# First norm of a two-layer backbone kernel on Trainium2: sum of squares, reciprocal and two tile splits ahead of the last scale tiles, the K/V block queued ahead of the last two tiles

## What is computed

```python
def rmsnorm(x, g):
    xf = x.astype(jnp.float32)
    y = xf * lax.rsqrt(jnp.mean(xf * xf, axis=-1, keepdims=True) + EPS)
    return (y * g.astype(jnp.float32)).astype(x.dtype)

def modulation(cond, w_mod, b_mod):
    m = jax.nn.silu(cond) @ w_mod + b_mod
    return jnp.split(m, 6, axis=-1)
...
        sh1, sc1, g1, sh2, sc2, g2 = [m[:, None, :] for m in modulation(c, w_mod[layer], b_mod[layer])]
...
        h = rmsnorm(x, norm1_g[layer]) * (1 + sc1) + sh1
        proj = h @ w_in_l
```

## Time and profile before

| | |
|---|---|
| median of three runs | 2337.09 us |
| profiled execution, own time | 2338.05 us |
| its span (first to last instruction) | 2336.3 us |
| TensorE busy in the span | 2217.6 us, 95% |
| VectorE busy | 1727.9 us, 74% |
| ScalarE busy | 1132.2 us, 48% |
| mean granted TensorE clock | 0.977 |
| data moved by DMA | 513.89 MB, mean 220 GB/s |

### The profile page before, as it was taken

How to read it: one execution, slowest core, us unless ns; L and a number is a source line. 1 busy time by engine, 2 the same in 40 slices (tenths; PEclk the granted TensorE clock), 3 DMA queues, 4 the chain that set the end, 5 groups by cost and what they waited for, 6 DMA issues and landing times.

```text
span 2336.3 us, 33202 instructions
## 1 busy us (share of the span) xinstructions
PE 2217.6 (95%) x12554; PEld 1868.1 (80%) x12554; DVE 1727.9 (74%) x2384; ACT 1132.2 (48%) x1502; POOL 42.7 (2%) x84
## 2 busy tenths in 40 slices
PE   7989999997999999789997999999999999999998
PEld 6754776655777777657986999999999999999997
DVE  6776587646666766776736888888888888888886
ACT  3315221213333232434324766767676666767675
POOL 0000000000000000000000000000000000000000
PEclk9998999999999999889997999999999999999999
DMA  7500144343444443312535898989898998989895
GB/s 302 183 30 1 68 155 161 127 144 119 160 152 162 144 144 126 116 43 78 183 123 215 318 355 306 361 303 359 311 353 325 337 359 303 361 303 358 311 348 194
DMA packets 61296, 513.89 MB, mean 220 GB/s; under 512 B 6963, under 2 KB 8115, under 8 KB 21045
## 3 DMA queue, kind: packets, MB, share of 16 engines
q1 hardware_dynamic: 49716, 471.16, 54.0%
q0 software_dynamic: 11520, 41.95, 5.0%
HBM read 512.03 MB, written 1.05 MB: 220 GB/s over the span
## 4 chain that ended last, share of the span: by engine, by line
PE 87%; DVE 7%; ACT 2%; issue 2%; DMA 1%; SPq 0%; DVEq 0%; ACTq 0%
PE bank L752 9%; PE bank L754 9%; PE bank L753 9%; PE bank L505 5%; PE bank L506 5%; PE bank L507 5%; PE bank L617 5%; PE bank L768 4%; PE bank L769 4%; PE bank L770 4%; PE bank L627 4%; PE bank L461 2%; PE bank L673 2%; PE bank L659 2%; PE bank L649 2%
## 5 line engine op out<-in xcount | busy, mean ns | idle before, releaser
L1448 DVE TENSOR_TENSOR m_low<-W,m_high 128x2048 fp32r<-128x2048 f32 x225 | 515.7, 2292 | 126.1 <-ACT m_high L1000 126.1
L752 PE MATMUL bank<-m_high,gathered_high 128*128 128x256 f32 x1792 | 508.7, 284 | 13.8 <-DVE m_low L1448 12.4
L754 PE MATMUL bank<-m_low,gathered_high 128*128 128x256 f32 x1792 | 507.7, 283 | 0.0
L753 PE MATMUL bank<-m_high,gathered_low 128*128 128x256 f32 x1792 | 507.0, 283 | 0.0
L1000 ACT ACTIVATE m_high<-W 128x2048 fp32r<-128x2048 f32 x225 | 431.9, 1920 | 8.2 <-issue 7.9
L752 PEld LDWEIGHTS bank<-m_high,gathered_high 128*128 128x128 f32 x1792 | 342.7, 191 | 25.2 <-DVE m_low L1448 14.8
L753 PEld LDWEIGHTS bank<-m_high,gathered_low 128*128 128x128 f32 x1792 | 342.7, 191 | 8.0
L754 PEld LDWEIGHTS bank<-m_low,gathered_high 128*128 128x128 f32 x1792 | 342.7, 191 | 0.0
L1451 DVE TENSOR_TENSOR m_low<-W,m_high 128x1024 fp32r<-128x1024 f32 x225 | 274.4, 1219 | 0.0
L505 PE MATMUL bank<-h_high,tile_high 128*128 128x512 f32 (+1 forms) x704 | 259.1, 368 | 11.7 <-DVE tile_low L1178 11.7
L1002 ACT ACTIVATE m_high<-W 128x1024 fp32r<-128x1024 f32 x225 | 237.2, 1054 | 6.8 <-PE bank L770 6.8
(11 more groups left out here) (216 smaller groups left out, 3559.2 us busy)
## 6 DMA issues: line engine op xcount, KB each, us to landing
W<-in_moe SPq DMA_DIRECT2D x225, 1536.0 KB, 8.3
W<-in_w_mod_later POOLq DMA_DIRECT2D x80, 512.0 KB, 3.6
W<-in_ffn SPq DMA_DIRECT2D x33, 1024.0 KB, 4.8
W<-in_attn_blocks SPq DMA_DIRECT2D x24, 1280.0 KB, 5.8
W<-in_attn_blocks SPq DMA_DIRECT2D x22, 1024.0 KB, 5.1
W<-in_attn_blocks SPq DMA_DIRECT2D x8, 1536.0 KB, 6.9
shift_tiles<-in_w_mod_first SPq DMA_DIRECT2D x8, 512.0 KB, 14.0
scale_tiles<-in_w_mod_first SPq DMA_DIRECT2D x8, 512.0 KB, 14.8
```

The lines of the kernel that those rows point to most:

```text
L752: mm(b[:, 0:256], hgh[:, k, :], m13h[:, u % 2, k, :], start=k == 0, stop=False)
L753: mm(b[:, 0:256], hgl[:, k, :], m13h[:, u % 2, k, :], start=False, stop=False)
L754: last = mm(b[:, 0:256], hgh[:, k, :], m13l[:, u % 2, k, :], start=False, stop=k == KD - 1)
L1448: tt(m13l[:, u % 2], chunk[u][:, 0:2 * D].rearrange("p (k n) -> p k n", k=KD), m13h[:, u % 2].bitcast(F32), ALU.subtract).then_inc(S("moe_ ...
```

## The change

1. SyncE queues block 0 (K and V) ahead of shift tile 7 and scale tile 7; at its old place, after scale tile 7, nothing is issued for it.
2. TensorE does `sum_squares` of the first norm after scale tile 5 instead of after tile 6.
3. VectorE adds the squares two at a time ahead of shift tiles 3, 4 and 5, instead of 5, 6 and 7.
4. VectorE no longer waits for the scale after shift tile 7. It goes on to `attention_half`, takes the reciprocal, splits tiles 0 and 1, and only then waits for `mod_scale_full`, adds the bias and makes the gain (`first_scale`).
5. ScalarE takes the root first and then makes the high parts of tiles 0 and 1.
6. Tile 2 (q0) is split after the norm's units on both engines, and ahead of clearing `ypad`. This holds in layer 1 as well, where tiles 0 and 1 stay ahead of the norm.

```diff
@@ SyncE @@
             for j in range(KD):
+                if j == KD - 1:
+                    sp.dma_start(slots[0][:, 0:BLOCK_LEN[0]], attn_in[0, 0, :, 0:BLOCK_LEN[0]]).then_inc(S("block_in0"), 16)
                 sp.dma_start(shift0[:, j], first_in[j]).then_inc(S(f"shift_tile_in{j}"), 16)
...
-                    sp.dma_start(slots[s][:, 0:n], attn_in[layer, idx, :, 0:n]).then_inc(S(f"block_in{s}"), 16)
+                    if layer or idx:
+                        sp.dma_start(slots[s][:, 0:n], attn_in[layer, idx, :, 0:n]).then_inc(S(f"block_in{s}"), 16)
@@ TensorE, modulation @@
-                    if j == KD - 2:
+                    if j == 5:
                         pe.wait_ge(S("cs_row_ready"), 4)
                         sum_squares(0, "norm1", T)
@@ ScalarE, norm @@
                 fn(root[:, 0:n], b[:, 0:n], ACT.Sqrt, bias=C("eps"), scale=1.0 / D).then_inc(free(layer, name), 1)
+                if layer == 0 and name == "norm1":
+                    for t in range(2):
+                        split(layer, t)
@@ ScalarE and VectorE, attention_half @@
-                for n in range(TILE_RING):
-                    split(layer, n)
+                if layer:
+                    for n in range(2):
+                        split(layer, n)
                 norm(layer, "norm1", T)
+                split(layer, 2)
@@ VectorE, modulation @@
-                    if j >= 5:
-                        for k in range(1 + 2 * (j - 5), 3 + 2 * (j - 5)):
+                    if 3 <= j < 6:
+                        for k in range(2 * j - 5, 2 * j - 3):
                             add_square(0, "norm1", k, T)
...
+                dve.wait_ge(S("mod_shift_ready"), KD)
+
+            def first_scale():
+
                 bias = vec[:, 0, KD:2 * KD].unsqueeze(2).broadcast_to([P, KD, 2])
                 dve.wait_ge(S("mod_scale_full"), 1)
                 tt(modT[:, 0, KD:2 * KD, :], banks[4][:, 0:2 * KD].rearrange("p (q v) -> p q v", v=2), bias, ALU.add) \
                     .then_inc(S("mod_scale_read"), 1)
                 dve.wait_ge(S("mod_scale_read"), 1)
-                dve.wait_ge(S("mod_shift_ready"), KD)
+                gains(0, "norm1")
@@ VectorE, norm @@
                 step(dve.reciprocal(rstd[:, 0:n], root[:, 0:n]))
+                if layer == 0 and name == "norm1":
+                    for t in range(2):
+                        split(layer, t)
+                    first_scale()
@@ VectorE, main @@
             modulation()
-            gains(0, "norm1")
```

## The result

The changed kernel is faster, and by more than forecast. Its median over seven runs is 2324.68 us, against 2337.09 us over seven runs of the kernel before in the same rounds: ratio 0.9957, 95% interval 0.9946 to 0.9969. (The two medians alone would give 0.9947; the ratio lies nearer to that of the means, 2327.2 and 2336.8 us, because the median falls into the faster of two groups.) Forecast were 2330.6 us, with a range down to 2328.6 us. The seven runs are not spread evenly, though. Four lie at 2324.06, 2324.23, 2324.61 and 2324.68 us, three at 2330.61, 2330.7 and 2331.5 us. Two later runs gave 2330.72 and 2330.9 us. Of nine runs of the same kernel four are near 2324.4 us and five near 2330.8 us, and the forecast hits the second group. So there are two things to explain: the start, and the 6.3 us between the groups.

A forecast was written before the change was run, and what follows sets the result against it. The start was taken to be bound by order: VectorE stood still 5.56 us for the last scale matmul. 6.7 us gained there less 0.2 us in layer 1 gave 6.5 us, median 2330.6 us, range 2328.6 to 2333.8 us.

The forecast's parts named there:

- The scale's wait is an order, not work; the first unit moves from 49.99 to 43.29 us: End of the start: splits and reciprocal need no scale, so the norm's first unit comes 6.70 us earlier.
- Nothing below 43.19 us is possible here: Norm's first unit: the scale's end at 42.53 us plus 0.66 us for bias and gain caps the gain at 6.8 us.
- TensorE's matmuls cost nothing more or less, the squares come 3 us early, the high parts hide behind the reciprocal: Start: scale still ends at 42.51 us, squares at about 29.2 us, ScalarE's high parts at 38.7 us with 1.6 us to spare.
- The two transfers delayed cost nothing: Start: shift tile 7 and scale tile 7 land behind block 0 with 0.8 and 4 us to spare, so zero cost.
- Tile 2 behind the norm, layer 0: Layer 0's first norm: tile 2 is ready for TensorE at 58.65 us, hidden before the pair's end at 59.32 us.
- the rival: Pair K and V: clock already up, q0 waits for tile 2 until 58.65 us; gain 7.2 us, 2329.9 us; chance 0.12.
- Layer 1: 0.2 us lost: Layer 1's first norm: tile 2 reaches TensorE at 968.4 instead of 968.19 us, costing 0.2 us, bounds 0 to 0.5 us.
- The sum, 6.5 us, and 2330.6 us: Whole kernel: 6.7 us gained at the start less 0.2 us in layer 1, median 2330.6 us, 0.28% less; chance 0.60.
- From the pair on nothing reads a clock on the wall: Everything behind the pair K and V: the gain at the start was taken to move all the rest along unchanged.
- My rival of the clock: Pair or a later stretch stays at 1.2 GHz longer: 2337.5 us for the whole pair, 2334 us for half; chance 0.10.
- one later low stretch shorter by its share: Lower end of the range, 2328.6 us: clock up at the pair, and one later stretch at 1.2 GHz shortened.
- three runs lay within 0.7 us: Argument against the rival of a slower kernel (chance 0.04), in which the clock is released later after the layers' pauses.

The follow-up runs named there:

- e7: Changed kernel with the fourth score matmul done three times in both attentions, block 0 queued after scale tile 7 as before; median 2318.45 us.
- e11: Changed kernel with the fourth score matmul done three times in both attentions, tile 2 of layer 0 split ahead of the norm; median 2319.7 us.
- e9_layer1_old_filled: Changed kernel with the fourth score matmul done three times in both attentions, layer 1's tile 2 split ahead of the norm; median 2318.17 us.
- e12: Changed kernel with two more 512-column matmuls behind the first sum of squares, into a bank nobody reads; six runs, 2318.62 to 2331.13 us, profiled at 2319.5 us.

## Why the prediction was right, and where it failed

- *The scale's wait is an order, not work; the first unit moves from 49.99 to 43.29 us.* Right: 42.57 and 42.61 us in two profiles, of which 0.5 us is the earlier shift tile and 0.25 us the bias and gain, taken too dear. "Nothing below 43.19 us is possible here" was wrong by the same two terms.
- *TensorE's matmuls cost nothing more or less, the squares come 3 us early, the high parts hide behind the reciprocal.* Right, except that the tiles got shorter in some runs; this paid nothing there, since VectorE came last.
- *The two transfers delayed cost nothing.* Right: shift tile 7 landed at 33.1 us and was taken up at 33.97 us, without a wait, and e7 is equal.
- *Tile 2 behind the norm, layer 0.* Right: hidden, and worth 1.2 us in the total against 1.0 reckoned (e11). Where the clock rose early, q0 came 0.05 us behind the low part of tile 2, as the rival had it, although the pair began at the low clock there too.
- *Layer 1: 0.2 us lost.* Not seen; in the profile of 2330.72 us q0 follows the pair without a gap at 960.97 us and the lead changes by less than 0.1 us, and e9_layer1_old_filled is 0.3 us faster, no difference. The order did not matter.
- *The sum, 6.5 us, and 2330.6 us.* Right in its mechanism for five of nine runs, whose clock pattern is that of the profiled kernel before. That these lie so close to 2330.6 us is partly luck. In equal patterns the profiles give 7.2 us, 0.7 us more than the sum, from the earlier tile and the cheaper gain; and the median that the sum was taken from mixed the runs near 2336.1 and 2338.2 us. The two errors cancel.
- *The step that failed* is this one: "From the pair on nothing reads a clock on the wall: blocks are loaded when a tile has been split, so a shift of the pair moves all the rest." It left out TensorE's clock. The rows already had a stretch at 0.51, and I took the other stretches as fixtures that move along. In four of nine runs, by their times, the one in layer 1's attention was missing (one of the four was profiled), worth 6.3 us; the median fell among them. My rival of the clock let it only stay low longer, and for a gain the range had no more than 1.3 us, "one later low stretch shorter by its share"; it ended 3.9 us too high. What the long stretches cost was to be had from windows over the attentions of the kernel before (13.7 us at 0.50 with TensorE the chain) and from the matmul pace at either level. That they can vanish was not to be seen in its one profile. What lets one vanish in one run and not in the next stays open.
- *"three runs lay within 0.7 us"* was used as proof that the clock's pattern is firm. It is nearly so for the kernel before, with two kinds of runs 2 us apart and one of 2330.68 us among 50, and not for the changed one.

The Trainium skill says on its page "TensorE: Matmul & The Clock Gate", section "What's actually happening", that the monitor behind the clock runs freely and does not start anew with the kernel, and that cold counts therefore vary from run to run. The two profiles of one kernel agree that the pace varies from run to run: 4.05 us against 6.83 us for the same 32 instructions. Whether a free-running monitor is the reason, no run here shows. The same section reckons the cost of the first ramp at under 1% of a typical kernel's span. One stretch in an attention, which is not that ramp, cost 6.3 us of 2331 us here, 0.27%, nearly as much as the change itself.

**The version that beats both.** The changed kernel with the pause filled: 2318.48 us, ratio 0.9916 (0.9902 to 0.9929) against the kernel before, all its runs below 2319 us. With layer 1 in the old order it is 2318.17 us, ratio 0.992 (0.9906 to 0.9933), which is the same. The filling alone (13.7 us off the kernel before) is worth nearly twice the reordering.

## What to carry to other kernels

When an engine waits for one operand of the next step, move up what needs other operands, and check which engine then ends last: here VectorE, by 0.1 us in the forecast and by 3.3 us where the scale tiles ran faster, so that a faster TensorE at the start brought nothing. Before you say that a saving early in a kernel moves everything behind it, list the stretches at low clock in which TensorE sets the pace, with their price; each can vanish or appear, and a few runs of the kernel before do not tell. Where TensorE pauses for a microsecond or two ahead of a long run of small matmuls, repeating one of them into the same bank can keep the clock up; here two repeats fitted into a pause of 2.04 us and delayed nothing.

## What the runs showed of the hardware

- One low stretch of 13.7 us in an attention costs 6.3 us (6.35 and 6.32 us where filling took it away). Runs of several kernels fall into groups at 2318.5, 2324.4 and 2331 us, and each profiled one agrees with its count of such stretches: none in 2319.5 us, one in 2324.06 us, two in 2330.72 us.
- In the kernel before, scale tiles 0 to 6, some 24 us of matmuls with 2 columns with one gap of 0.44 us, kept a pace of 3.45 us a tile. That is 1.2 GHz, for behind the sum of squares two tiles took half as much in some executions (3.63 us in e12, 4.05 us in that of 2324.06 us). The rows of the latter have a granted clock of 1.00 from 34.5 to 37.7 us and of 0.50 from 37.8 to 48.0 us, and the tiles ran until 38.86 us, so TensorE was not idle before the clock fell:

```profile
34.50:37.70 3.20, 3.20 (x29) 2.96 (x27) 3.17 (x5) 2.58 (x3) 0.92 (x2) 1.00 1.04 438
37.80:48.00 10.20, 4.01 (x13) 3.37 (x13) 9.92 (x19) 3.23 (x7) 0.16 (x1) 0.50 0.84 322
```

- The clock column reads 1.00 for the first 58 us of the kernel before, also where the pair's spacing of 0.43 us shows 1.2 GHz. Ahead of the first change of the clock, the spacing is the measure, not the column.
